# RWKV recurrence on one Trainium2 core: TensorE's side work cut into smaller pieces and laid into both gaps of every level of the inverse

## The reference, cut to what matters

```python
def step(state, inp):
    r_t, w_t, k_t, v_t, a_t, b_t = inp
    sa = jnp.einsum("bhvk,bhk->bhv", state, a_t)
    state = (state * w_t[:, :, None, :] + sa[..., None] * b_t[:, :, None, :]
             + v_t[..., None] * k_t[:, :, None, :])
    return state, jnp.einsum("bhvk,bhk->bhv", state, r_t)
```

## Time and profile before

| | us |
|---|---|
| median of 3 runs | 5182.35 |
| lowest and highest | 5178.41, 5202.02 |
| the profiled execution, its own time | 5185.3 |
| its span in the profile | 5183.5 |
| TensorE busy, whole span | 4500.0 (87%) |
| VectorE, ScalarE, GpSimd busy | 1936.2, 1543.6, 405.6 |
| first seed of pass 0, first seed of pass 8, start of the recurrence's last read | 1661.1, 1942.5, 1982.6 |

### The profile page before, as it was taken

The page is one execution under the profiler, slowest core; times in us unless marked ns, Lnnn a source line. Parts: engine busy times, 40 slices in busy tenths (PEclk is TensorE's granted clock), DMA queues, the critical chain, the costliest instruction groups (busy, mean ns, idle before and its releaser), DMA issues. The chain is left out here.

```text
span 5183.5 us, 75408 instructions
## 1 busy us (share of the span) xinstructions
PE 4500.0 (87%) x29222; PEld 3653.8 (70%) x29222; DVE 1936.2 (37%) x2951; ACT 1543.6 (30%) x2760; POOL 405.6 (8%) x345
## 2 busy tenths in 40 slices
PE   4977887977796996979689899999978878999998
PEld 4966787965793885857543678888757656788887
DVE  2543432444323555131334343334332155433333
ACT  1352223233223333221157432222322233322221
POOL 0004310012000110000023100000100000000001
PEclk6998998998896998989899999999989979999999
DMA  2101011111210002111100111111101121111112
GB/s 76 45 21 42 2 26 50 45 49 51 75 39 32 11 7 107 42 63 37 29 23 16 33 45 49 49 49 49 46 28 40 41 62 40 45 48 47 47 49 70
DMA packets 355347, 223.59 MB, mean 43 GB/s; under 512 B 28291, under 2 KB 336291, under 8 KB 355125
## 3 DMA queue, kind: packets, MB, share of 16 engines
q1 hardware_dynamic: 355124, 220.42, 14.7%
HBM read 175.48 MB, written 24.02 MB: 38 GB/s over the span
## 5 line engine op out<-in xcount | busy, mean ns | idle before, releaser
L2462 PE MATMUL ffp_acc<-ff_m_hi_rounded,ffp_w_hi_rounded 128*128 128x512 f32 x1024 | 399.2, 390 | 0.4 <-DVE ff_m_rounded L2532 0.3
L2462 PE MATMUL ffp_acc<-ff_m_rounded,ffp_w_hi_rounded 128*128 128x512 f32 x1024 | 398.8, 389 | 0.0
L2462 PE MATMUL ffp_acc<-ff_m_hi_rounded,ffp_w_rounded 128*128 128x512 f32 x1024 | 398.8, 389 | 0.0
L2462 PE MATMUL ffp_acc<-ff_inner_hi_rounded,ffp_w_hi_rounded 128*128 128x512 f32 x1024 | 398.3, 389 | 0.0
L2462 PE MATMUL ffp_acc<-ff_inner_hi_rounded,ffp_w_rounded 128*128 128x512 f32 x1024 | 398.3, 389 | 0.0
L2462 PE MATMUL ffp_acc<-ff_inner_rounded,ffp_w_hi_rounded 128*128 128x512 f32 x1024 | 398.3, 389 | 0.0
L2473 ACT ACTIVATE ffp_w_hi_rounded<-ffp_w 128x256 fp32r<-128x256 f32 x512 | 189.7, 409 | 445.7 <-DMA ffp_w<-w_mlp_dram 219.0
L2528 DVE TENSOR_TENSOR ffp_w_rounded<-ffp_w,ffp_w_hi_rounded 128x256 fp32r<-128x256 f32 x512 | 217.3, 462 | 134.0 <-ACT ffp_w_hi_rounded L2473 128.8
L2462 PEld LDWEIGHTS ffp_acc<-ff_m_hi_rounded,ffp_w_hi_rounded 128*128 128x128 f32 x1024 | 192.7, 188 | 43.5 <-issue 3.5
L2462 PEld LDWEIGHTS ffp_acc<-ff_m_hi_rounded,ffp_w_rounded 128*128 128x128 f32 x1024 | 192.6, 188 | 40.0
L2462 PEld LDWEIGHTS ffp_acc<-ff_m_rounded,ffp_w_hi_rounded 128*128 128x128 f32 x1024 | 192.5, 188 | 40.0
(11 more groups left out here) (648 smaller groups left out, 10308.5 us busy)
## 6 DMA issues: line engine op xcount, KB each, us to landing
ffp_w<-w_mlp_dram SPq DMA_DIRECT2D x256, 128.0 KB, 2.2
ffp_w<-w_up_dram SPq DMA_DIRECT2D x128, 128.0 KB, 2.2
ffp_w<-w_down_dram SPq DMA_DIRECT2D x128, 128.0 KB, 2.3
pa_w<-w_in_dram SPq DMA_DIRECT2D x72, 128.0 KB, 2.5
pb_w<-w_in_dram SPq DMA_DIRECT2D x68, 128.0 KB, 2.5
p1o_w<-w_out_dram SPq DMA_DIRECT2D x32, 256.0 KB, 4.3
b1o_mix<-mix SPq DMA_DIRECT2D x16, 512.0 KB, 10.9
mamba_stage<-b_pool SPq DMA_DIRECT2D x9, 896.0 KB, 5.5
```

The source lines that it names most:

```text
L2462: mm = nc.tensor.matmul(acc[s][:, c, :], rounded(a[:, s, k, :]), rounded(b[:, k, at]), start=(k == 0 and i == 0), stop=(k == KD - 1 and i ...
```

## The change

The same instructions are done on the same data; the places where they stand are others, and four things are cut up.

- TensorE: `decays` is cut in two (in front of the second seed, and gap A of level 1), `solve` in two (gap B of level 1, gap A of level 2), the outputs of `results` in two (gap A of levels 3 and 4). The state's growth is a function of its own, `grow`, in gap A of level 5 (in the last pass behind all levels). The transpose of the values comes first, in gap B of level 2. `scores` 0 and 1 go to gap B of levels 4 and 5, `scores` 2 to gap A of level 6, `scores` 3 and two transposes behind the joins of level 6.
- ScalarE does the exponentials in three pieces at levels 1 and 2, each with its own semaphore step. GpSimd's `scaled_b` waits for the first piece alone.
- VectorE scales in three pieces at levels 2 and 3; `read_scores` 0 stands behind the masks of level 5, `read_scores` 1 behind those of level 6, 2 and 3 at the end; `next_state` moves from level 3 to level 5.
- The values, transposed, live in a tile of their own (`vt`, three buffers), and seven of the constant matrices are loaded with 64 columns instead of 128.

```diff
-        names = ["ident", "upto_mid", "before_mid", "before", "upto", "turned0", "ident64"] + [f"near{l}" for l in range(1, LAST)]
-        mt = part.sb("mats", [P, len(names), P])
+        whole = ["ident", "upto_mid", "before_mid", "before", "upto"]
+        narrow = ["turned0", "ident64"] + [f"near{l}" for l in range(1, LAST)]
+        names = whole + narrow
+        mt, mn = part.sb("mats", [P, len(whole), P]), part.sb("narrow", [P, len(narrow), 64])
...
-        tok = [part.sb(f"tok{s}", [P, 3, F, P]) for s in range(2)]
+        tok = [part.sb(f"tok{s}", [P, 2, F, P]) for s in range(2)]
+        vt = [part.sb(f"vt{s}", [P, F, P]) for s in range(3)]
...
-            def decays(t):
-                pe.wait_ge(S["lw_in"], 16 * (t + 1))
-                if t >= 1:
-                    pe.wait_ge(S["scores_read"], F * t)
-                for f in range(F):
+            def decays(t, f0):
+                if f0 == 0:
+                    pe.wait_ge(S["lw_in"], 16 * (t + 1))
+                    if t >= 1:
+                        pe.wait_ge(S["scores_read"], F * t)
+                for f in (f0, f0 + 1):
                     mm = M(prep[:, f // 2, 256 * (f % 2):256 * (f % 2) + 256], lw[:, f, :], both("upto_mid"), start=True, stop=True)
-                mm.then_inc(S["decays"], 1)
+                if f0:
+                    mm.then_inc(S["decays"], 1)
...
             def turn(t, i):
-                what = (bt, kt, b[:, 8:12, at(t)])[i]
+                what = (b[:, 8:12, at(t)], bt, kt)[i]
                 if i == 0 and t >= 2:
-                    pe.wait_ge(S["state_sum"], t - 1)
-                if i == 1 and t >= 2:
+                    pe.wait_ge(S["rhs_read"], t - 1)
+                if i == 1:
+                    if t >= 2:
+                        pe.wait_ge(S["state_sum"], t - 1)
+                    else:
+                        pe.wait_ge(S["tokens"], 3 * t + 1)
+                if i == 2 and t >= 2:
                     pe.wait_ge(S["stored"], t - 1)
-                if i == 2:
-                    pe.wait_ge(S["tokens"], 3 * t + 1)
                 for f in range(F):
-                    mm = nc.tensor.transpose(per_pair(late[:, i % 2, :])[:, f, :], what[:, f, :], mat("ident"))
+                    mm = nc.tensor.transpose(per_pair(late[:, (0, 0, 1)[i], :])[:, f, :], what[:, f, :], mat("ident"))
                 mm.then_inc(S["turned"], 1)
...
-            def right_side(t):
-                v = by_head(tok[t % 2][:, 2])
+            def right_side(t, f0):
+                v = by_head(vt[t % 3][:, :, :])
                 out = per_head(late[:, 0, :])
-                pe.wait_ge(S["tokens"], 3 * min(t + 2, NT1))
-                pe.wait_ge(S["scores_read"], F * (t + 1))
-                pe.wait_ge(S["hm_done"], t + 1)
-                for f in range(F):
+                if f0 == 0:
+                    pe.wait_ge(S["tokens"], 3 * min(t + 1, NT1 - 1) + 2)
+                    pe.wait_ge(S["scores_read"], F * (t + 1))
+                    pe.wait_ge(S["hm_done"], t + 1)
+                for f in (f0, f0 + 1):
                     M(per_pair(late[:, 0, :])[:, f, :], ar[t % 3][:, f, 0, :], hmz[t % 2][:, f, :, :], start=True, stop=False, skip_group_check=True)
                     for h in (2 * f, 2 * f + 1):
                         mm = M(out[:, h, :], kp[t % 2][:, h, 0, :], v[:, h, :], start=False, stop=True, skip_group_check=True)
...
+            def grow(t):
+                pe.wait_ge(S["u_read"], t + 1)
+                if t + 2 < NT1:
+                    pe.wait_ge(S["tokens"], 3 * (t + 2) + 1)
+                for f in range(F):
+                    M(per_pair(late[:, 0, :])[:, f, :], tok[t % 2][:, 0, f, :], u[:, 2 * f:2 * f + 2, :], start=True, stop=False)
+                    mm = M(per_pair(late[:, 0, :])[:, f, :], tok[t % 2][:, 1, f, :], vt[t % 3][:, f, :], start=False, stop=True)
+                mm.then_inc(S["grown"], 1)
+
...
             pe.wait_ge(S["loaded"], 16 * len(names))
-            decays(0)
+            decays(0, 0)
+            decays(0, 2)
+            turn(0, 0)
             for f in range(F):
                 scores(0, f)
-            for i in range(3):
-                turn(0, i)
+            turn(0, 1)
+            turn(0, 2)
             for t in range(NT1):
-                more = t + 1 < NT1
+                more, late_part = t + 1 < NT1, t >= 1
                 inv.seed(pe, t, 0)
-                if t >= 1:
-                    right_side(t - 1)
+                if late_part:
+                    right_side(t - 1, 0)
+                    right_side(t - 1, 2)
+                if more:
+                    decays(t + 1, 0)
                 inv.seed(pe, t, 1)
                 for l in range(1, LEVELS):
                     inv.multiply(pe, t, l, 0)
                     inv.multiply(pe, t, l, 1)
-                    if l == 2:
-                        if t >= 1:
-                            solve(t - 1)
-                        if more:
-                            decays(t + 1)
-                    if l == 3 and t >= 1:
-                        results(t - 1)
-                    if l >= 4 and more:
-                        scores(t + 1, l - 4)
-                        turn(t + 1, l - 4)
+                    if l == 1 and more:
+                        decays(t + 1, 2)
+                    if l == 2 and late_part:
+                        solve(t - 1, 4)
+                    if l == 3 and late_part:
+                        results(t - 1, 0)
+                    if l == 4 and late_part:
+                        results(t - 1, 2)
+                    if l == 5 and late_part and more:
+                        grow(t - 1)
+                    if l == 6 and more:
+                        scores(t + 1, 2)
                     inv.join(pe, t, l, 0)
                     inv.join(pe, t, l, 1)
-                if more:
-                    scores(t + 1, 3)
-            right_side(NT1 - 1)
-            solve(NT1 - 1)
-            results(NT1 - 1)
+                    if l == 1 and late_part:
+                        solve(t - 1, 0)
+                    if l == 2 and more:
+                        turn(t + 1, 0)
+                    if l in (4, 5) and more:
+                        scores(t + 1, l - 4)
+                    if l == 6 and more:
+                        scores(t + 1, 3)
+                        turn(t + 1, 1)
+                        turn(t + 1, 2)
+                if late_part and not more:
+                    grow(t - 1)
...
-            def exps(t):
-                act.wait_ge(S["decays"], t + 1)
-                if t >= 1:
-                    act.wait_ge(S["scaled"], t)
-                    act.wait_ge(S["scaled_b"], t)
-                A(e3, cum[:, :, 0, :], ACT.Exp, scale=-1.0)
-                A(e1, cum[:, :, 0, :], ACT.Exp)
-                A(e2, cum[:, :, 1, :], ACT.Exp)
-                A(em[t % 3][:, :], cum[:, :, 1, 0], ACT.Exp, scale=-1.0)
-                A(ed[t % 3][:, :], cum[:, :, 0, P - 1], ACT.Exp).then_inc(S["exps"], 1)
+            def exps(t, i):
+                if i == 0:
+                    act.wait_ge(S["decays"], t + 1)
+                    if t >= 1:
+                        act.wait_ge(S["scaled"], t)
+                        act.wait_ge(S["scaled_b"], t)
+                    A(e3, cum[:, :, 0, :], ACT.Exp, scale=-1.0).then_inc(S["exps"], 1)
+                elif i == 1:
+                    A(e1, cum[:, :, 0, :], ACT.Exp).then_inc(S["exps"], 1)
+                else:
+                    A(e2, cum[:, :, 1, :], ACT.Exp)
+                    A(em[t % 3][:, :], cum[:, :, 1, 0], ACT.Exp, scale=-1.0)
+                    A(ed[t % 3][:, :], cum[:, :, 0, P - 1], ACT.Exp).then_inc(S["exps"], 1)
...
                 inv.take(act, copy, t, 0, 1)
                 for l in range(1, LEVELS):
-                    if l == 2 and t >= 1:
-                        take(per_head(late[:, 1, :]), u, "u_done", "u_read", t - 1)
-                    if l >= 4 and more:
-                        token(t + 1, l - 4)
                     inv.take(act, copy, t, l, 0)
                     if l >= LAST - 1:
                         inv.take(act, copy, t, l, 1)
+                    if l in (1, 2) and more:
+                        exps(t + 1, l - 1)
+                    if l == 2 and t >= 1:
+                        take(per_head(late[:, 1, :]), u, "u_done", "u_read", t - 1)
                     if l == 2 and more:
-                        exps(t + 1)
-                    if l == 3 and t >= 1:
+                        token(t + 1, 0)
+                        exps(t + 1, 2)
+                    if l == 4 and t >= 1:
                         take(per_pair(late[:, 1, :]), unit_k[:, :, at(t - 1)], "outputs", "stored", t - 1)
+                    if l == 6 and more:
+                        token(t + 1, 1)
+                        token(t + 1, 2)
...
-                pool.wait_ge(S["exps"], t + 1)
+                pool.wait_ge(S["exps"], 3 * t + 1)
...
-            def scaled(t):
```

(61 more changed lines are left out.)

48 lines of the change are left out of this document (25 added, 23 removed).

## The result

The changed kernel takes 5228.56 us (median of 10 runs, 5207.98 to 5247.76) against 5188.92 us of the kernel before (10 runs, 5178.41 to 5204.67): ratio 1.0062, 95% interval 1.0046 to 1.0079. It is slower, by some 40 us where 13.6 were forecast, and lies above the range (5181 to 5212). The base of the forecast, 5182.35 (3 runs), was itself 6.6 us under the median of the ten.

The account below looks back on a forecast made before the run. TensorE's order was the bound. Per pass +1.0 seams, -1.7 waits removed, +2.6 new waits, taken as +1.8, so +12.6 us over seven passes; ends -1, -1, +3: 5182.35 + 13.6 = 5196 us, range 5181 to 5212.

Parts of the forecast that it names:

- (a): TensorE's order in a pass: five more seams between multiplies and 128-row work, +1.0 us a pass (0.5 to 1.5).
- (b): Gaps of levels 1, 2, 4 and between 5 and 6: waits removed by work placed there, -1.7 us a pass.
- (c): Level 6: scores 2 waits 1.9 us and scores 3 0.9 us for VectorE's readings, taken as +2.6 a pass.
- The overlap of 0.2: New waits at level 6: 0.1 us off at each of two places for pipelined VectorE instructions, 2.8 to 2.6.
- Mamba's 1.42 us busy of 3.40 at full clock: Evidence against the clock falling in each pass: a Mamba window with TensorE busy 1.42 of 3.40 us showed 1.00 throughout.
- (d): The ends of the stage: pass 0 -1 us, before the first scores -1, last pass +3.
- Pass 0: First pass: -3.2 wait, -1.5 half clock, +1.3 cut scalings, +2.6 new waits, together -1 us (rounded).
- The prelude: Before the first scores: GpSimd and VectorE start behind the first exponential instead of behind five, -1 us.
- Last pass: Last pass: right_side waits about 2.5 us for next_state, less about 0.2, plus 0.7 for partly half-clocked work: +3 us.
- The port: Rival, level 2: scaled 0 late by a GpSimd multiply, take overruns by 0.5 to 1.0 a pass, 5200 to 5203; chance 0.15.
- The three amounts: Range below 5196: free outgoing seams 3.5 us, shorter new waits 3.5, lowest earlier run 4 under the median; given as 5181.
- the clock rival: Level 6: clock falls in each pass, 3.4 us at half clock, at most 1.7 us, 13.6 over eight passes, 5210; chance 0.2.

Follow-up runs that it names:

- run 9: Changed kernel with scores 0, 1, 2 one level earlier, readings at levels 4 to 6, one turn at level 6, last-pass growth at level 5: ratio 0.9990.
- run 3: Changed kernel with matmuls without use filling both level 6 waits, ahead of scores 2 and scores 3: ratio 1.0033.
- run 4: Changed kernel with matmuls without use in the first level 6 wait alone, ahead of scores 2: ratio 1.0035.
- run 5: Kernel before with only VectorE's order changed: reading of scores 1 behind level 6's masks, of scores 2 behind the first begin: ratio 1.0089, 5240.5 us.
- run 6: Changed kernel with grow and next_state at level 5 in the last pass too: ratio 1.0031.
- run 7: Changed kernel with the reading of scores 1 ahead of level 6's masks, and grow and next_state at level 5 in the last pass: ratio 0.9992.
- run 2: Changed kernel with the reading of scores 1 moved ahead of level 6's two masks on VectorE: ratio 1.0012.
- run 1: Changed kernel with scores 0, 1, 2 and their readings back at levels 4, 5 and 6: ratio 1.0001.

## Why the prediction was wrong

*(a), (b) Seams and waits removed.* Forecast -0.7 a pass together; measured 37.42 - 35.85 = 1.57, less the new waits by starts (2.98 - 1.07 = 1.91 and 1.95 - 1.07 = 0.88), gives -1.2. Right in kind, half a microsecond too dear; the pass of run 9, 34.62 at full clock with no wait at the scores, gives the same -1.2.

*(c) New waits.* Right: 1.91 and 0.88 against "a wait of 1.9" and "a wait of 0.9", at L1484, released by L1708. The overlap of 0.2 that I took off was not there. Net +1.57 a pass against 1.8.

*The step that failed* is in the rivals: "3.4 us at half clock are at most 1.7 us", with a chance of 0.2 for a fall in each pass. The mechanism that I set aside is what took place, in six of eight passes, and a fall inside the passes lasted 10.2 us and cost 3.6, twice the price. The price came from the half-clock windows of rows 11, the only falls in this stage before, each taken at its own length of 3.4 to 3.5; how long a fall behind another wait lasts they could not say, and I should have kept a longer one as the upper bound. Elsewhere in the trace of before, too, each half-clock stretch with TensorE over 90% busy lasted 3.4 us; the longer ones had it busy 85% at most. So 10.2 us at a busy TensorE is what only the runs show. The case against it, Mamba's 1.42 us busy of 3.40 at full clock, was one window; that the clock kept up once shows only that it can, as passes 3 and 7 do here. And I overlooked the nearest rows for the rival. In the delta rule, which uses `LevelInverse` too, TensorE of the kernel before stands eight times for 1.67 us in front of a seed, waiting for VectorE's L1037, and behind seven of these waits the clock falls, 0.3 to 1.4 us after their end. Windows before and behind the first such fall, in the kernel before:

```profile
444.90:448.30 3.40, 1.73 (x39) 1.40 (x39) 3.03 (x5) 0.67 (x3) 1.97 (x3) 1.00 0.00 0
448.40:451.80 3.40, 3.40 (x18) 3.40 (x18) 0.97 (x2) 0.86 (x2) 2.46 (x3) 0.50 0.02 5
```

By these rows a wait of 1.9 us was likely to cost the clock, and 0.2 was too low.

In passes 1 to 7 the sum is 280.8 us against 251.0: 11 us are the order at full clock (new waits 19.5, less 8.5 gained) and 19 the clock, and the forecast had 12.6 and nothing.

The Trainium skill ("TensorE: Matmul & The Clock Gate", Part 1) ties the fall to long idle gaps and would have let these short ones pass; the trace disagrees, with falls inside waits of 1.84 us, and so do runs 3 to 5.

*(d) The ends.* Pass 0: forecast -1, measured +1.8, because the clock fell there too (8.1 us of half clock before the pass ends) and -1.5 had been put down for its absence. The half clock of the prelude, over at 1660.1 before, also reaches 3.7 us into the pass here (1659.6 to 1663.3), which no term had. The prelude: -1 forecast, -1.5 measured. Last pass: +3 forecast, +6.8 measured; the 2.5 us wait was right, but "work that already ran partly at half clock, +0.7" was a fall of its own that reached to the end of the stage, 15.0 us against 3.4. Runs 6 and 7 give this term 8.4 and 8.8 us.

*The port.* The rival was false. The scaling of `kt` does take 1.42 to 1.43 us instead of 0.685 beside GpSimd in passes 1 to 7 (0.71 in pass 0), but in pass 3 VectorE then still waits 0.39 us for the join, so the take is not late:

```profile
1785.92 1.42 DVE L1696 TENSOR_TENSOR rwkv_kt<-b_pool,rwkv_e 128x512 f32<-128x512 f32 x1
1787.73 0.69 DVE L1027 COPY rwkv_xx<-rwkv_inv 128x512 f32<-128x512 f32 x1 [0.39 <-PE rwkv_inv L1017]
```

*The range.* The three amounts that were to carry it down from 5196 (3.5, 3.5 and 4 us) reach 5185, not 5181; it makes no difference to the outcome, which lies 17 us over the upper end. There the clock rival, priced at 13.6 us for eight falls, set the bound; the falls cost 19 us in passes 1 to 7 alone.

*What is left over.* The sum of the profiled executions is 13.6 forecast against 41.8: +19 clock in passes 1 to 7, +3.8 last pass, +2.8 pass 0, -1.6 for the seams, -0.5 prelude, and 4.8 behind the stage, whose cause stays open. Why passes 3 and 7 kept their clock stays open too.

## What to carry to other kernels

When work moves into the gaps of one engine, move what empties its buffer on the other engine with it: here one reading placed behind two masks cost 1.91 us a pass, and putting it ahead of them gave most of the loss back. Price a new wait on TensorE twice, as its length and as a chance of half clock behind it, taking for the second a stretch of several times the wait; filling such a wait with matmuls without use is a quick test that parts the two. Look for falls behind waits of that length in the whole trace of before, not only in the stage that changes. A loop's last turn, where a late piece has nothing left to hide it, deserves its own line in the sum.

## What the runs showed of the hardware

- A single wait of TensorE of 1.84 us, between stretches that are over 95% busy, took the clock to 1.2 GHz in six of eight passes (changed kernel), three of eight (run 6) and all of them (run 5), inside the wait or up to 1.6 us behind its end; one of 1.67 us did so seven times out of eight (delta rule, kernel before). A wait of 0.8 us did so in none of passes 1 to 7 of the profiled executions of runs 2, 4 and 7.
- Once down, it stayed there for 6.8 to 13.7 us in the passes, and for 23.9 us behind the last pass's 2.4 us wait (2004.6 to 2028.5), though TensorE was over 95% busy in the windows of the passes (9.76 and 9.86 of 10.20 us above). In the delta rule of the kernel before it stayed down for 3.4 us each time.
- The same code, with the same waits of 0.7 us at most, kept its clock in the last pass of run 7 and lost it in that of run 9; at the 2.4 us wait of the last pass it held in run 4 and fell in the changed kernel and runs 1, 2 and 3.
